# A hybrid encoder layer on one core: each tile's modulation chunk in quarters between the rounds of the inverse

## The reference, cut to what matters

```python
def trunk_layer(x, c, ...):
    mod = (jax.nn.silu(c) @ w_ada + b_ada)[:, None, :]
    sh1, sc1, g1, sh2, sc2, g2 = jnp.split(mod, 6, axis=-1)
    h = layer_norm(x) * (1 + sc1) + sh1
    ...
    x = layer_norm(ALPHA * x + (1 + g1) * mix, ln1_g, ln1_b)
    h = layer_norm(x) * (1 + sc2) + sh2
    ...

def chunk_gated_delta(q, k, v, g, beta, s0):
    ...
    A = jnp.where(strict, jnp.einsum('bhnid,bhnjd->bhnij', k_beta, k) * dmask, 0.0)
    T = lax.linalg.triangular_solve(eye + A, jnp.broadcast_to(eye, A.shape), left_side=True, lower=True)
    u = T @ v_beta
    w = T @ (k_beta * jnp.exp(decay)[..., None])
    ...
    def step(S, inp):
        v_new = u_n - w_n @ S
        o_n = qd_n @ S + qk_n @ v_new
        S = S * gl_n[..., None, None] + jnp.einsum('bhck,bhcv->bhkv', kd_n, v_new)
        return S, o_n
```

## Time and profile before

| | us |
|---|---|
| median of 3 runs | 1379.94 |
| their range | 1379.54 to 1380.66 |
| the profiled execution | 1379.55 |
| its span, first to last instruction | 1377.7 |
| PE busy | 1334.2 (97%) |
| DVE busy | 945.0 (69%) |
| ACT busy | 578.7 (42%) |
| POOL busy | 563.9 (41%) |

### The profile page before, as it was taken

The page is one execution under the profiler, slowest core; times in us unless marked ns, Lnnn a source line. Parts: engine busy times, 40 slices in busy tenths (PEclk is TensorE's granted clock), DMA queues, the critical chain, the costliest instruction groups (busy, mean ns, idle before and its releaser), DMA issues.

```text
span 1377.7 us, 29023 instructions
## 1 busy us (share of the span) xinstructions
PE 1334.2 (97%) x10724; PEld 1220.2 (89%) x10724; DVE 945.0 (69%) x1477; ACT 578.7 (42%) x1278; POOL 563.9 (41%) x622
## 2 busy tenths in 40 slices
PE   6999999999999999999999999999999999999997
PEld 4899999998978888887899999999999998887675
DVE  6516786965378887788796766555666558676398
ACT  6523344346476666254632333333333325443120
POOL 4987868683033334132234334434234334000041
PEclk9999999999999999999999999999999999999998
DMA  9422344344356564522314543545534458996894
GB/s 347 133 92 61 108 107 119 105 118 148 103 164 205 193 193 140 171 91 83 86 49 155 194 159 123 171 135 184 191 129 134 162 177 327 359 370 241 286 322 178
DMA packets 184406, 234.61 MB, mean 170 GB/s; under 512 B 17709, under 2 KB 118641, under 8 KB 184305
## 3 DMA queue, kind: packets, MB, share of 16 engines
q1 hardware_dynamic: 180128, 221.36, 49.5%
q10 hardware_dynamic: 4176, 11.89, 2.2%
HBM read 170.29 MB, written 61.73 MB: 168 GB/s over the span
## 4 chain that ended last, share of the span: by engine, by line
PE 58%; DVE 8%; ACT 3%; issue 3%; DMA 2%; POOL 1%; POOLq 0%; ACTq 0%; SPq 0%; DVEq 0%
PE bank L2557 30%; PE bank L2471 11%; PE bank L308 3%; PE bank L1826 2%; PE bank L1187 2%; PE bank L2488 1%; ACT hp L1933 1%; PE bank L1202 1%; PE bank L1253 1%; DMA rW<-w_down 1%; DVE stat L1966 1%; DVE xt L2003 1%; PE bank L1863 1%; PE bank L1244 1%; DVE split L2600 1%
## 5 line engine op out<-in xcount | busy, mean ns | idle before, releaser
L2471 PE MATMUL bank<-split 128*128 128x512 f32 x924 | 212.0, 390 | 2.3 <-DVE split L2604 2.3
L2471 PEld LDWEIGHTS bank<-split 128*128 128x128 f32 x924 | 172.7, 188 | 43.8 <-DVE split L2600 4.1
L2557 PE MATMUL bank<-Tlo,rh 128*128 128x272 f32 x640 | 184.7, 289 | 0.0
L2557 PE MATMUL bank<-Thi,rh 128*128 128x272 f32 x640 | 184.2, 288 | 0.0
L2557 PE MATMUL bank<-Thi,rl 128*128 128x272 f32 x640 | 184.0, 288 | 0.0
L308 PE MATMUL bank<-hT_hi,whi 128*128 128x384 f32 (+1 forms) x504 | 166.0, 329 | 1.2 <-ACT urow L3159 0.9
L308 PE MATMUL bank<-hT_hi,wlo 128*128 128x384 f32 (+1 forms) x504 | 164.3, 326 | 0.0
L308 PE MATMUL bank<-hT_lo,whi 128*128 128x384 f32 (+1 forms) x504 | 164.2, 326 | 0.0
L2557 PE MATMUL bank<-hT_lo,rh 128*128 128x272 f32 x480 | 138.5, 289 | 0.0
L2557 PE MATMUL bank<-hT_hi,rl 128*128 128x272 f32 x480 | 138.4, 288 | 0.0
L2557 PE MATMUL bank<-hT_hi,rh 128*128 128x272 f32 x480 | 137.9, 287 | 0.0
(11 more groups left out here) (463 smaller groups left out, 3273.7 us busy)
## 6 DMA issues: line engine op xcount, KB each, us to landing
wada<-w_ada SPq DMA_DIRECT2D x12, 2048.0 KB, 9.1
raw<-w_up SPq DMA_DIRECT2D x40, 512.0 KB, 5.1
wsum<-w_down SPq DMA_DIRECT2D x11, 1024.0 KB, 5.6
wt<-wsum SPq DMA_DIRECT2D x11, 1024.0 KB, 4.0
rW<-wt SPq DMA_DIRECT2D x44, 256.0 KB, 6.6
split<-split SPq DMA_DIRECT2D x22, 512.0 KB, 5.0
wraw<-w_in SPq DMA_DIRECT2D x21, 512.0 KB, 4.3
rows<-convrow ACTq DMA_DIRECT2D x16, 577.5 KB, 3.5
```

The lines of the kernel that those rows point to most:

```text
L2471: last = pe.matmul(ps[down_bank(q, r)][:], a[:, rows], w, start=(k == 0 and m == 0), stop=(k == KH - 1 and m == 2))
L2557: last = pe.matmul(ps[banks[c]][:, 0:NC], w[:, ks], a, start=(n < 3 and k == 0 and p == 0), stop=(k == 3 and p == 2), skip_group_check=True)
```

## The change

`ada_rows` is cut into four calls of `ada_part(t, k)`: each takes one r and one half of the 512 columns (256), that is four products of 128x32 weights with 256 columns instead of eight with 512 for a whole chunk. For t = 1 to 7 the call behind the scores goes away, and the four parts stand in the rounds of tile t: k = 0 between P and X of round 0, k = 1 ahead of P of round 1, k = 2 between P and X of round 1, and k = 3 ahead of P of round 2. Chunk 0 stays where it was, as four parts in a row. The waits for the load and for bank 5 stand ahead of part 0, and the signal `ada_mm` behind part 3. On DVE the addition `mod_rows(t)` moves for t = 1 to 7 from behind the growth of round 0 to the head of round 2, ahead of `whole_last`.

```diff
--- before.py
+++ after.py
@@ -1207,8 +1207,12 @@
             def round_of(t, r):
 
                 units = [(u, l) for u, l in ((t, ROUNDS + r), (t + 1, r)) if 0 <= u < TILES and l <= top(u)]
+                if t and r:
+                    ada_part(t, 2 * r - 1)
                 for u, l in units:
                     level_P(u, l)
+                if t and r < ROUNDS - 1:
+                    ada_part(t, 2 * r)
                 for u, l in units:
                     level_X(u, l)
 
@@ -1245,14 +1249,21 @@
                     pe.matmul(h4(4)[:, h, :], QK[x][:, h, :], Vb[:, h, :], start=False, stop=True)
                     pe.matmul(kv_of(h), kdec[t % 3][:, h, :], Vb[:, h, :], start=True, stop=True).then_inc(on["g_kv"], 1)
 
+            def ada_part(t, k):
+
+                r, half = k % 2, slice(k // 2 * (ADA_N // 2), (k // 2 + 1) * (ADA_N // 2))
+                if k == 0:
+                    pe.wait_ge(on["ada"][t % 2], 16 * (t // 2 + 2))
+                    pe.wait_ge(on["g_vp"], min(t + AHEAD_OF, TILES))
+                for q in range(4):
+                    last = pe.matmul(ps[5][32 * q:32 * q + 32, half], csil4b[:, 4 * r + q, 2 * (CHUNKS - 1 - t):2 * (CHUNKS - 1 - t) + 32], wada2[:, t % 2, 4 * r + q, half],
+                                     start=(r == 0), stop=(r == 1))
+                if k == 3:
+                    last.then_inc(on["ada_mm"], 1)
+
             def ada_rows(t):
-                pe.wait_ge(on["ada"][t % 2], 16 * (t // 2 + 2))
-                pe.wait_ge(on["g_vp"], min(t + AHEAD_OF, TILES))
-                for r in range(2):
-                    for q in range(4):
-                        last = pe.matmul(ps[5][32 * q:32 * q + 32, :], csil4b[:, 4 * r + q, 2 * (CHUNKS - 1 - t):2 * (CHUNKS - 1 - t) + 32], wada2[:, t % 2, 4 * r + q, :],
-                                         start=(r == 0), stop=(r == 1))
-                last.then_inc(on["ada_mm"], 1)
+                for k in range(4):
+                    ada_part(t, k)
 
             def gate_rows(pair, out):
 
@@ -1351,8 +1362,6 @@
                     gate_rows(6, ps[5][0:16, 2 * P:3 * P]).then_inc(on["gate_R"], 1)
                 if more:
                     scores(n)
-                if t + 1 < PTILES:
-                    ada_rows(t + 1)
             pe.wait_ge(on["g_S"], TILES * HEADS)
             return turn_o
 
@@ -1720,6 +1729,8 @@
                 n = t + AHEAD_OF
                 more = n < TILES
                 for r in range(ROUNDS):
+                    if t and r == ROUNDS - 1:
+                        mod_rows(t)
                     if r < ROUNDS - 1:
                         grow_X0(t, ROUNDS + r)
                         grow_X0(t + 1, r)
@@ -1728,7 +1739,7 @@
                     else:
                         whole_last(t)
                         grow_X(t + 1, r)
-                    if r == 0:
+                    if r == 0 and not t:
                         mod_rows(t)
                     if r == 1 and t:
                         out_rows(t - 1)
```

## The result

| | before | changed |
|---|---|---|
| median, us | 1379.94 | 1392.32 |
| range of 3 runs each | 1379.54 to 1380.66 | 1391.15 to 1393.55 |
| profiled execution | 1379.55 | 1393.55 |
| its span | 1377.7 | 1391.6 |

The ratio of the times is 1.009, with a 95% interval of 1.0075 to 1.0105: 12.4 us slower. In a later series the changed kernel ran at 1397.55 us beside 1380.95 us, a ratio of 1.0121 (1.0104 to 1.0139), 16.6 us.

The account below looks back on a forecast made before the run. The prediction took PE's queue and P's wait for DVE as ending together; removal gives 0.0, quarters cost 1.65 us in six tiles and 1.3 in one, 11.2 on 1379.55, plus 0.4 for the median: 1391.1 us, range 1388 to 1393.5.

Parts of the forecast that it names:

- The bound: Round 0: P's second half waits for DVE's first_level, starting 0.14 to 0.15 us behind it; PE's queue ends together with this wait.
- The removal: Taking the chunk from behind the scores gives 0.0 us a tile; PE idles some 1.7 us instead.
- The first rival: P's second half does not wait, so the removal gives 1.95 us a tile: 1377.8 or 1371.9 us; chance 0.06.
- The quarters: Four parts in the rounds, 0.66 us each with edges, cost 1.65 us a tile in six tiles and 1.3 in tile 7.
- the gaps: PE's gaps between P and X and ahead of rounds 1 and 2 cover 0.18, 0.33, 0.16 and 0.32 us of the quarters.
- The edges of 0.23 us: Each quarter between 64x64 products pays 0.10 us ahead of it and 0.13 us behind, besides 0.43 us of columns.
- the second rival: Quarters overlap with the 64x64 products and cost their columns alone, 0.8 us a tile: 1385.5 us; chance 0.09.
- The full drain of the fourth: Each quarter waits for the modelled end of the product before it, 2.2 us a tile: 1395 us; chance 0.10.
- The moved addition: The 0.68 us addition on DVE at the head of round 2 costs 0.0 us, at most 0.05 a tile.
- the third rival: PE's idle stretch halves its clock, up to 1.7 us each, at three or four of seven borders: 1397 us; chance 0.15.
- the two rows: Profile stretches of 3.40 us: PE busy 1.34 was followed by half the clock, busy 2.04 was not.
- The upper end of the forecast: With the late copy on DVE and 0.04 us more at each edge of a tile, the time is 1393.5 us.

Follow-up runs that it names:

- the filled kernel: Changed kernel plus three quarter-sized filler products in PE's wait ahead of P's second half, round 0: 1390.52 us (ratio 1.0069), later 1388.14 (1.0053).
- The single quarters: Changed kernel with parts 0 to 2 in PE's wait in round 0, part 3 at round 2's head (1387.3 us) or between P and X of round 1 (1387.19).
- edges alone: Changed kernel with 16 columns instead of 256 in each of the four parts for chunks 1 to 7: 1385.59 us, ratio 1.0042.
- two halves: Changed kernel with two parts in a row at the heads of rounds 1 and 2, none between P and X: 1389.97 us, ratio 1.0064.

## Why the prediction was right, and where it was not

- **The bound: right. The removal: right but for 0.17 us a tile.** The second half of P waits for DVE. All seven second halves of the changed kernel start 0.10 or 0.15 us behind L1658, after 1.64 to 1.69 us idle (forecast 1.7), and the kernel without the chunk gains no more than 3.5 us of 13. The first rival falls with this. Borders are 19.5 to 19.7 us apart at full clock (forecast 19.4 to 19.9), 20.8 with a stretch at half the clock. What the forecast missed is that an early first half of P lets X start sooner: the stretch without quarters is then 4.3 us and not 4.46.
- **The quarters: right against the kernel before, in part by an offset.** Forecast 1.65 us a tile; measured 6.15 - 4.46 = 1.69 in the filled kernel, and 11.2 us over seven tiles in the changed one, after the clock's part. In the filled kernel the delay against the kernel before grows by 0.53 us up to the first X, by 0.33 up to P of round 1, by 0.50 up to its X and by 0.33 up to round 2; the forecast was 0.48, 0.33, 0.50 and 0.34. But against 4.3 us the four quarters cost 1.86 us of their 2.64, so the gaps cover less than the 0.99 us forecast, and the missed 0.17 us of the removal makes up for it. The single quarters show the same. The edges of 0.23 us held. The overlap of the second rival would make the stretch 5.3 us and did not come. The full drain of the fourth would make it 6.6 us; by the Trainium skill's rule on a change of tiling mode (TensorEngine Tiling, Key Properties) the array drains, and the trace agrees that each change costs something, but less than up to the modelled end.
- **The moved addition: right.** No cost shows. In tile 7 it took away the 0.38 us by which round 2 was late before; the stretch there is 1.4 us longer in the filled kernel (forecast 1.3).
- **The clock: wrong in weight.** It was the third rival, with 0.15, and not in the sum. It came in five of seven tiles in both profiles of the changed kernel, where the rival took three or four. Its mechanism was as described, idle PE ahead of round 0; a stretch costs 1.44 to 1.50 us and not 1.7. That part of it falls on gaps would explain this and was not tested. The step that failed is the judgement from the two rows: a tile with 1.7 us idle was said to be between them and, by the chance it got, was counted as nearer to the one that keeps its clock. Busy 1.71 of 3.40 us was between 1.34 and 2.04, and the clock fell. The comparison was no guide at all: in the kernel with the chunk in the wait it fell behind a stretch that was busy 2.41.
- **The number: right in part by offsets.** 1391.1 was forecast and 1392.32 measured. In the profile, where 11.2 us were forecast and 13.9 measured, these are 11.2 of quarters and 7.4 of clock, less 2.4 outside the rounds, less 2.9 ahead of the recurrence, and 0.6 behind it. The 2.9 us come from the front, ahead of every changed instruction; without them the profiled execution would have taken 1396.5 us, where 1390.8 was forecast for it. In the later series the same kernel took 1397.55, at the range's upper end, near what the third rival gave (1397). The upper end of the forecast adds up to 1391.1 + 2.2 + 0.35 = 1393.7 and not 1393.5; nothing hangs on it.
- **The rest of a tile: missed.** From round 2 to the next border I expected no change; it is 13.2 us in nearly every tile with four quarters in the rounds, idle or filled, where it was 13.3 to 14.2. Pauses put down to "issue" are 0.9 of the 2.4 us; the other 1.5 us are not resolved. These pauses went away there and come back, longer, in the kernels with the chunk in the wait, at the same places of PE's instruction stream. What PE lacks in a pause is open.

## What to carry to other kernels

Work that fills an engine's wait for another engine costs almost nothing there, however long its rows; ask which semaphore the next instruction waits for before taking it out. Work put into the gaps of a chain that is bound by its own latency costs its length and its edges less what the gap covers, each time it is cut; and the gaps themselves can change with the edit, so measure the kernel with the gaps empty too. An idle stretch made on PE can cost twice, since the clock may fall behind it; a filler shows which part of a loss that is. Pauses in which nothing is waited for are worth counting by their place in the instruction stream before they are put down to the work around them.

## What the runs showed of the hardware that was not expected

- PE idle for 1.64 to 1.69 us in each tile, with work around it, brought half the clock in 5, 5, 2 and 1 of seven tiles (the changed kernel twice, edges alone, two halves); idle for 1.47 to 1.52 us it brought none of seven, in a kernel that has no quarters either. One such stretch made the 4.7 to 6.15 us behind it 1.3 to 1.5 us longer.
- After idle time, the second half of P starts 0.10 us behind its releaser in every second tile and 0.15 us in the others.
- A change between 64x64 and 128x32 tiles of the array and back costs about 0.23 us together, with 16 columns as with 256.
- PE pauses of 0.2 to 1.9 us, in which the profile shows nothing waited for, stood a multiple of 256 PE instructions apart, at the same places in every trace that had them, whatever work stood there.
